# Row tiles of the router added on another engine, a gather's indices read one item early, and a first preparation over more accumulators, in a two-layer hybrid decoder step

## The chip, the cores and the metric

The kernel runs on one core of one Trainium2 chip. Its engines are TensorE (PE), VectorE (DVE), ScalarE (ACT), GpSimd (POOL) and SyncE (SP), each with a queue of its own. The metric is device time of one launch in microseconds (us), less is better; two kernels are compared in runs on the same chip.

## The reference, cut to what matters

Two decoder layers over 1024 prompt tokens and 64 sample tokens (1088 in all) of width 1024. Each layer mixes tokens, then applies a channel mixer, then adds a gated input embedding. The channel mixer of the second layer is a mixture of 8 experts of which each token takes 2, and the change lies just ahead of it and in it:

```python
def _moe_swiglu(x, w_router, wg, wu, wd):
    ...
    logits = jnp.dot(xt.astype(jnp.float32), w_router.astype(jnp.float32))
    top_v, top_i = lax.top_k(logits, TOP_K)
    top_w = jax.nn.softmax(top_v, axis=-1)
    flat_e = top_i.reshape(-1)
    order = jnp.argsort(flat_e)
    tok = order // TOP_K
    xs = xt[tok]
    sizes = jnp.bincount(flat_e, length=N_EXPERTS).astype(jnp.int32)
    h = jax.nn.silu(lax.ragged_dot(xs, wg, sizes)) * lax.ragged_dot(xs, wu, sizes)
    ys = lax.ragged_dot(h, wd, sizes) * top_w.reshape(-1)[order][:, None].astype(x.dtype)
    y = jnp.zeros_like(xt).at[tok].add(ys)
```

All arithmetic is float32. The kernel keeps an operand of a large product as two parts, a high one rounded to TensorE's faster float32 form (fp32r) and the low rest, and adds three products (high by high, low by high, high by low).

## The kernel before, in words

Activations live transposed in SBUF: `XHI` and `XLO` (high and low part) are 128 partitions by 8 column groups of the width by 1088 tokens. The five queues run on their own and meet at semaphores only; `wait_ge(sem, n)` holds the whole queue in which it stands. Each queue's order is written out by hand, layer by layer.

**Layer 0 and the mixing of layer 1** take the first half of the time. The mixer's last step in layer 1 leaves the new `XHI`, `XLO` block by block (three blocks of 384, 384 and 320 tokens, `BLOCKS`); VectorE's `finish_x` writes the last of it.

**Routing.** TensorE multiplies the three blocks by the router (`logits(0)`, `logits(1)`, then the sums of squares by `stats`, then `logits(2)`; lines 987 and 988). VectorE copies each block's logits into `LGT` (line 2271) and turns the sums into row scales in between (`norm_tokens`, lines 1725 to 1728, `scale_ready`). The same tokens are needed as rows in memory, since the experts gather them by row: for each of 9 row tiles of 128 tokens (the last has 64), GpSimd adds `XHI` and `XLO` into `XF` (line 630; 7 buffers, so the last two adds wait until earlier tiles have left, and each add counts up `xf_ready`), TensorE transposes the eight 128x128 pieces of `XF` into two PSUM banks (`rows`, line 1003), ScalarE scales them into `ROWT` (line 1495) and sends them to `token_rows` (line 1498). TensorE's order is: rows of tiles 0 and 1, logits per token (line 1017), rows 2 to 4, a wait for `counts_ready` and the running counts (lines 1024 to 1026), rows 5 to 8, the ranks of the first expert's tokens (line 1033), the list of items (line 1037). VectorE meanwhile finds the two best experts (lines 2278 to 2288), casts and compares (2291, 2294), adds up (to `counts_ready`), then finds which expert comes first (`first_known`, line 2330, on which SyncE issues the first two loads of expert weights, line 417), a mask (line 2339) and the token numbers `IDS` (`ids_ready`). When all rows are written and `IDS` is there, GpSimd gathers the first item's 336 rows in three indirect DMAs (line 635, `xg_ready`), and after that scatters the sorted token numbers to `sorted_tokens` (line 643).

**First preparation.** `prepare(k)`, for each of 8 column groups: TensorE transposes three pieces of the gathered rows `XG` into one PSUM bank (line 1051), ScalarE writes the high part `XSH` with the norm's gain as scale (line 1517), VectorE the low part `XSL` (line 2426) and frees the bank. These banks are the two miscellaneous ones (6 and 7), so TensorE is at most two groups ahead. The six main banks (0 to 5, `open_bank`, freed by `evicted`) are not used here.

**Items.** A loop of 8 items (expert by expert, 336 rows at most; the sizes of the product come from a table) does gate, up and down products: lines 704 to 706 for gate and up, 817 to 819 for down. The first product waits for each `k` of the preparation by itself (`splits`). Each item prepares the next one's rows in its last two down steps. GpSimd's loop (lines 650 to 660) fetches the rows of the item after that: it waits for `xg_used` (the preparation has read `XG`), then reads token numbers into `IDX` by three DMAs (line 656), waits for them, then gathers (line 660).

Of the kernel before, what the change touches and what calls it, by code (L numbers as in the profile page):

```python
# [18 lines left out]
F32 = mybir.dt.float32  # L19
# [3 lines left out]
ALU = mybir.AluOpType  # L23
ACT = mybir.ActivationFunctionType
AXX = mybir.AxisListType.X

P = 128
# [6 lines left out]
NT = -(-NTOK // P)  # L34
# [104 lines left out]
def build(nc, A, O):  # L139
# [5 lines left out]
    def at(name, shape, dt, off):  # L145
        return nc.alloc_sbuf_tensor_at(name, list(shape), dt, offset=off)
# [141 lines left out]
    IDX = at("IDX", [P, len(XBLK), 4], I32, PH + 80288)  # L288
    assert PH + 80336 <= END
    o = [PH + 73984]  # L290
# [72 lines left out]
    def tokens(j):  # L363
        return min(P, NTOK - j * P)
# [29 lines left out]
    def spacer(eng):  # L394

        eng.sem_inc(S["spacer"], 1)
# [132 lines left out]
    def _(g):  # L529
# [94 lines left out]

        g.wait_ge(S["split_done"], W_MOE)
        for j in range(NT):
            n = tokens(j)
            if j >= len(XF):
                g.wait_ge(S["evicted"], Q_MIX1 + 24 + 2 * (j - len(XF) + 1))
            g.tensor_tensor(XF[j % len(XF)][:, :, 0:n], XHF[:, :, j * P:j * P + n], XLF[:, :, j * P:j * P + n], ALU.add).then_inc(S["xf_ready"], 1)  # L630

        g.wait_ge(S["rows_written"], 16 * NT)
# [17 lines left out]
        with g.Fori(0, SLOTS) as it:  # L650
            with g.If(it < n_items):
                row = g.value_load(ITEMS[0:1, bass.ds(it + L_ROW + 2, 1)], min_val=0, max_val=PAIRS)
                g.wait_ge(S["xg_used"], it + 1)
                spacer(g)
                for j, (r0, n) in enumerate(XBLK):
                    g.dma_start(IDX[0:n, j, :], XS[bass.ds(row + r0, n), :]).then_inc(S["idx_ready"], 16)
                g.wait_ge(S["idx_ready"], it * 48 + 48)
                spacer(g)
                for j, (r0, n) in enumerate(XBLK):
                    g.indirect_dma_start(XG[0:n, j, :], None, XR[0:NTOK, :], bass.IndirectOffsetOnAxis(ap=IDX[0:n, j, 0:1], axis=0)  # L660
                                         ).then_inc(S["xg_ready"], 16)
# [17 lines left out]
    def _(pe):  # L679
# [166 lines left out]
        for l in range(DEPTH):  # L846
# [128 lines left out]
            else:  # L975
# [20 lines left out]
                def rows(j):  # L996

                    n = tokens(j)
                    pe.wait_ge(S["xf_ready"], j + 1)
                    for h in range(2):  # L1000
                        b = open_bank()
                        for k in range(4):
                            ins = pe.transpose(PS[0:n, b, k * P:(k + 1) * P], XF[j % len(XF)][:, 4 * h + k, 0:n], IDF[:])
                        ins.then_inc(q.next(), 1)
# [13 lines left out]
                ins.then_inc(m.next(), 1)  # L1018
                for j in range(2, 5):
                    rows(j)  # L1020
# [5 lines left out]
                pe.matmul(PS[:, b, NT * NE:(NT + 1) * NE], ONES[:], TM[:, NT - 1, :], start=True, stop=True).then_inc(m.next(), 1)  # L1026
                for j in range(5, NT):
                    rows(j)
# [94 lines left out]
                for k in range(KC):  # L1123
                    prepare(k)
                turn = nc.alloc_registers("pe_expert", engines=[pe.engine])
# [139 lines left out]
    def _(act):  # L1265
# [117 lines left out]
        for l in range(DEPTH):  # L1383
# [103 lines left out]
            else:  # L1487
# [59 lines left out]
                with nc.body("act_further", valid_engines=[act.engine]):  # L1547
# [14 lines left out]
                    act.br("act_firsts")  # L1562
                nc.switch_bb("act_firsts")
                for k in range(KC):
                    prepare(k)
                with act.Fori(0, NE) as e:
# [106 lines left out]
    def _(dve):  # L1673
# [262 lines left out]
        for l in range(DEPTH):  # L1936
# [327 lines left out]
            else:  # L2264

                for j, (t0, n) in enumerate(BLOCKS):
                    if j == 2:
                        norm_tokens()
                        dve.sem_inc(S["scale_ready"], 1)
                    ps = misc_ready()  # L2270
                    v.do(dve.tensor_copy(LGT[:, t0:t0 + n], ps[0:2 * NE, 0:n]), m)
                v.sync()
                dve.sem_inc(S["logits_ready"], 1)
                v.do(dve.memset(LG[:], 0.0))
                v.sync()
# [31 lines left out]
                assert step_ >= NT and whole is TM  # L2307
                dve.sem_inc(S["counts_ready"], 1)

                wide_e = lambda t: t.unsqueeze(1).to_broadcast([P, NT, NE])  # L2310
# [110 lines left out]

                def prepare(k):

                    dve.wait_ge(S["split_hi"], split.at(split.n + 1))
                    spacer(dve)
                    v.do(dve.scalar_tensor_tensor(XSL[:, k, :], PS[:, 6 + m.n % 2, 0:CAP], gain(3)[:, k:k + 1], XSH[:, k, :].bitcast(F32),  # L2426
                                                  ALU.mult, ALU.subtract), m)
                    v.sync()
                    dve.sem_inc(split.next(), 1)  # L2429
                    if k == KC - 1:  # L2430
                        dve.sem_inc(S["split_req"], KC)
                        sreq.n += KC
                        dve.sem_inc(S["xg_used"], 1)
# [64 lines left out]
                for k in range(KC):  # L2498
                    prepare(k)
                with dve.Fori(0, NE) as e:  # L2500
# [125 lines left out]
```

## Time and profile before, and how to read it

| what | value |
|---|---|
| median of 3 runs | 5123.61 us (5120.17 to 5128.44) |
| the profiled execution, its own time | 5115.6 us |
| its span, from first to last instruction | 5114.0 us |
| mean granted TensorE clock | 0.982 |
| PE busy, share of the span | 4951.5 us, 97% |
| DVE busy | 3363.5 us, 66% |
| ACT busy | 1587.4 us, 31% |
| POOL busy | 449.8 us, 9% |

The profiled execution is 1.6 us longer than its span, and 8.0 us under the median of the runs. Busy time leaves out waits, branches and DMA issues; a busy PE is not a PE at its peak. "Idle before" is what an engine stood still ahead of a group, with what ended that wait behind the arrow. A q behind an engine's name (SPq, ACTq, DVEq) means its queue, not its datapath. Where a time line merges several instructions of one line into one row, its duration runs from the first's start to the last's end, and short pauses are within it. The granted clock is a share of 2.4 GHz: 1.00 is 2.4 GHz, 0.50 is 1.2 GHz, and what lies between is a mean over a stretch that has both.

### The profile page before, as it was taken

To read this page: it belongs to the slowest core of one execution; us is meant where nothing else is said; L and a number is where in the kernel's file an instruction comes from. 1 tells how busy PE (TensorE), PEld (TensorE's weight loads), DVE (VectorE), ACT (ScalarE), POOL (GpSimd) and SP (SyncE) were. 2 spreads that over 40 slices of the span, in tenths; PEclk is the share of its full clock that TensorE was granted. 3 is DMA by queue.
4 is the path that set the end of the run, shared out by engine and by line. 5 is a ranking of instruction groups with operands and counts; after the bars stand their busy time and mean duration, and the time that the engine had idled before them with its cause. 6 is when DMAs were issued, how large, how long until landed. Compare 5 with 4: busy or idle time off the path is not lost.

```text
span 5114.0 us, 86952 instructions
## 1 busy us (share of the span) xinstructions
PE 4951.5 (97%) x33265; PEld 4891.5 (96%) x33266; DVE 3363.5 (66%) x5241; ACT 1587.4 (31%) x2281; POOL 449.8 (9%) x288
## 2 busy tenths in 40 slices
PE   8999999999999999999979999999999999999988
PEld 8999999999998999999969999999999999999988
DVE  5677756444556756876557777666667777876655
ACT  2112122111113311122234434333334444443333
POOL 3110101110102021110030000000000000000020
PEclk9999999999999999999989999999999999999989
DMA  3111111111111111111025554444445555554431
GB/s 105 44 45 41 41 40 42 50 41 41 49 42 44 41 56 40 47 41 42 30 89 200 173 174 164 159 143 159 152 150 194 192 184 184 190 183 155 145 128 42
DMA packets 397849, 521.90 MB, mean 102 GB/s; under 512 B 13192, under 2 KB 353654, under 8 KB 397512
## 3 DMA queue, kind: packets, MB, share of 16 engines
q1 hardware_dynamic: 358320, 459.63, 27.3%
q10 hardware_dynamic: 29272, 33.08, 1.9%
q0 software_dynamic: 9920, 24.85, 1.6%
q8 instruction: 193, 3.16, 0.3%
q14 instruction: 144, 1.18, 0.1%
HBM read 494.91 MB, written 22.60 MB: 101 GB/s over the span
## 4 chain that ended last, share of the span: by engine, by line
PE 53%; DVE 4%; issue 3%; DMA 2%; ACT 1%; DVEq 0%; ACTq 0%; POOL 0%; SPq 0%; POOLq 0%
PE PS L704 12%; PE PS L706 12%; PE PS L705 12%; PE PS L817 4%; PE PS L818 4%; PE PS L819 4%; DMA WRAW<-in_moe_w_up 1%; PE PS L1237 1%; PE PS L753 1%; PE PS L755 1%; PE PS L754 1%; ACT WHI L1285 0%; PE PS L1062 0%; DVE WLO L1685 0%; DVE XSL L2426 0%
## 5 line engine op out<-in xcount | busy, mean ns | idle before, releaser
L1685 DVE TENSOR_TENSOR WLO<-WRAW,WHI 128x1024 fp32r<-128x1024 f32 x866 | 1071.5, 1238 | 364.8 <-ACT WHI L1285 243.9
L704 PE MATMUL PS<-XHI,WHI 128*128 128x384 f32 (+1 forms) x3648 | 1203.0, 330 | 10.7 <-DVE XLO L1942 4.5
L706 PE MATMUL PS<-XHI,WLO 128*128 128x384 f32 (+1 forms) x3648 | 1197.9, 328 | 0.0
L705 PE MATMUL PS<-XLO,WHI 128*128 128x384 f32 (+1 forms) x3648 | 1196.8, 328 | 0.0
L1285 ACT ACTIVATE WHI<-WRAW 128x1024 fp32r<-128x1024 f32 x866 | 899.1, 1051 | 915.5 <-PE PS L819 604.8
L704 PE MATMUL PS<-XSH,WHI 128*128 128x232 f32 (+6 forms) x3584 | 1061.9, 296 | 13.3 <-DVEq L2429 9.9
L706 PE MATMUL PS<-XSH,WLO 128*128 128x232 f32 (+6 forms) x3584 | 1057.6, 295 | 0.0
L705 PE MATMUL PS<-XSL,WHI 128*128 128x232 f32 (+6 forms) x3584 | 1057.3, 295 | 0.0
L704 PEld LDWEIGHTS PS<-XHI,WHI 128*128 128x128 f32 x3648 | 691.7, 190 | 12.9 <-issue 5.2
L704 PEld LDWEIGHTS PS<-XSH,WHI 128*128 128x128 f32 x3584 | 681.8, 190 | 15.3 <-DVEq L2429 13.8
L705 PEld LDWEIGHTS PS<-XLO,WHI 128*128 128x128 f32 x3648 | 691.4, 190 | 0.9
L706 PEld LDWEIGHTS PS<-XHI,WLO 128*128 128x128 f32 x3648 | 690.5, 189 | 0.0
L706 PEld LDWEIGHTS PS<-XSH,WLO 128*128 128x128 f32 x3584 | 681.7, 190 | 0.0
L705 PEld LDWEIGHTS PS<-XSL,WHI 128*128 128x128 f32 x3584 | 681.4, 190 | 0.0
L817 PE MATMUL PS<-EHI,WHI 128*128 128x232 f32 (+6 forms) x1792 | 532.1, 297 | 2.8 <-DVE EACC L2477 1.7
L818 PE MATMUL PS<-ELO,WHI 128*128 128x232 f32 (+6 forms) x1792 | 524.8, 293 | 0.0
L819 PE MATMUL PS<-EHI,WLO 128*128 128x232 f32 (+6 forms) x1792 | 524.7, 293 | 0.0
L579 POOL TENSOR_TENSOR WRAW<-WRAW,PAR 128x2048 f32<-128x2048 f32 x78 | 286.2, 3670 | 2311.1 <-DMA WRAW<-in_w_in 1097.2
L2477 DVE TENSOR_TENSOR EACC<-PS,EACC 128x336 f32<-128x336 f32 x832 | 373.0, 500 | 43.0 <-PE PS L819 16.1
L1329 ACT ACTIVATE T<-T 128x384 f32<-128x384 f32 (+1 forms) x240 | 121.8, 508 | 761.7 <-DVEq L1808 761.5
L817 PEld LDWEIGHTS PS<-EHI,WHI 128*128 128x128 f32 x1792 | 338.8, 189 | 5.5 <-DVE EACC L2477 3.0
L818 PEld LDWEIGHTS PS<-ELO,WHI 128*128 128x128 f32 x1792 | 338.9, 189 | 0.0
(402 smaller groups left out, 5973.6 us busy)
## 6 DMA issues: line engine op xcount, KB each, us to landing
WRAW<-in_moe_w_gate SPq DMA_DIRECT2D x112, 1024.0 KB, 5.0
WRAW<-in_moe_w_up SPq DMA_DIRECT2D x112, 1024.0 KB, 5.0
WRAW<-in_moe_w_down SPq DMA_DIRECT2D x112, 1024.0 KB, 4.9
WRAW<-in_w_in SPq DMA_DIRECT2D x48, 1024.0 KB, 5.2
WRAW<-in_ffn_w_gate SPq DMA_DIRECT2D x11, 1024.0 KB, 5.3
WRAW<-in_ffn_w_up SPq DMA_DIRECT2D x11, 1024.0 KB, 5.3
WRAW<-in_ffn_w_down SPq DMA_DIRECT2D x11, 1024.0 KB, 5.0
expert_rows<-YT ACTq DMA_DIRECT2D x18, 512.0 KB, 3.9
```

Source lines behind the costliest of these rows:

```text
L579: g.tensor_tensor(w, w, gain(norm).unsqueeze(2).to_broadcast([P, KC, DB]), ALU.mult).then_inc(S["folded"], 1)
L704: pe.matmul(PS[:, bank, 0:n], wh, hi(k), start=(k == 0), stop=False)
L705: pe.matmul(PS[:, bank, 0:n], wh, lo(k), start=False, stop=False)
L706: ins = pe.matmul(PS[:, bank, 0:n], wl, hi(k), start=False, stop=(k == KC - 1))
L753: pe.matmul(PS[:, b, 0:n], wh[:, k, :], Y[0][:, k, t0:t0 + n], start=(k == 0), stop=False)
L817: pe.matmul(PS[:, b, 0:n], WHI[s][:, d, :], hi[:, f, t0:t0 + n], start=(f == 0), stop=False)
L818: pe.matmul(PS[:, b, 0:n], WHI[s][:, d, :], lo[:, f, t0:t0 + n], start=False, stop=False)
L819: ins = pe.matmul(PS[:, b, 0:n], WLO[s][:, d, :], hi[:, f, t0:t0 + n], start=False, stop=(f == 1))
L1285: act.activation(WHI[halves.n % HL][:], raw_view(tile % RAW, half, kind), ACT.Copy).then_inc(halves.next(), 1)
L1329: serve(lambda: act.activation(t[:, 0:n], t[:, 0:n], ACT.Sigmoid))
L1685: v.do(dve.tensor_tensor(WLO[s][:], raw_view(conv.n // 2 % RAW, conv.n % 2, kind), WHI[s][:].bitcast(F32), ALU.subtract), conv)
L2477: v.do(dve.tensor_tensor(a, ps[:, 0:CAP], a, ALU.add), q)
```

## The change

Three edits, all around the experts of layer 1.

1. The sums `XHI + XLO` for row tiles 0 to 6 leave GpSimd's queue and are formed by VectorE (`row_sums`), put between its own steps: 0 to 2 each ahead of a block's logits, 3 ahead of `norm_tokens`, 4 and 5 behind `logits_ready`, 6 behind `counts_ready`. Tiles 7 and 8 get no sum: TensorE forms each piece itself by two accumulating products with the identity, `XHI` first and then `XLO`. Rows of tile 4 move behind the running counts.
2. The first preparation uses the six main banks for groups 0 to 5 and the two miscellaneous ones for 6 and 7. ScalarE runs a one-column activation of the preparation's kind (`SCRAP`) ahead of it.
3. GpSimd's loop reads the token numbers into `IDX` as soon as the previous gather has landed, and waits for `xg_used` only ahead of the gather.

```diff
+    SCRAP = at("SCRAP", [P, 1], F32, PH + 80352)
...
@@ GpSimd
-        g.wait_ge(S["split_done"], W_MOE)
-        for j in range(NT):
-            n = tokens(j)
-            if j >= len(XF):
-                g.wait_ge(S["evicted"], Q_MIX1 + 24 + 2 * (j - len(XF) + 1))
-            g.tensor_tensor(XF[j % len(XF)][:, :, 0:n], XHF[:, :, j * P:j * P + n], XLF[:, :, j * P:j * P + n], ALU.add).then_inc(S["xf_ready"], 1)
...
-                g.wait_ge(S["xg_used"], it + 1)
+                g.wait_ge(S["xg_ready"], it * 48 + 48)
                 spacer(g)
                 for j, (r0, n) in enumerate(XBLK):
                     g.dma_start(IDX[0:n, j, :], XS[bass.ds(row + r0, n), :]).then_inc(S["idx_ready"], 16)
                 g.wait_ge(S["idx_ready"], it * 48 + 48)
+                spacer(g)
+                g.wait_ge(S["xg_used"], it + 1)
                 spacer(g)
@@ TensorE, rows
-                    pe.wait_ge(S["xf_ready"], j + 1)
+                    summed = j < len(XF)
+                    if summed:
+                        pe.wait_ge(S["xf_ready"], j + 1)
                     for h in range(2):
                         b = open_bank()
                         for k in range(4):
-                            ins = pe.transpose(PS[0:n, b, k * P:(k + 1) * P], XF[j % len(XF)][:, 4 * h + k, 0:n], IDF[:])
+                            if summed:
+                                ins = pe.transpose(PS[0:n, b, k * P:(k + 1) * P], XF[j][:, 4 * h + k, 0:n], IDF[:])
+                            else:
+                                for X in (XHI, XLO):
+                                    ins = pe.matmul(PS[0:n, b, k * P:(k + 1) * P], X[:, 4 * h + k, j * P:j * P + n], IDR[:], start=(X is XHI), stop=(X is XLO))
...
-                for j in range(2, 5):
+                for j in range(2, 4):
                     rows(j)
                 pe.wait_ge(S["counts_ready"], 1)
...
-                for j in range(5, NT):
+                for j in range(4, NT):
                     rows(j)
@@ TensorE, first preparation
                 for k in range(KC):
-                    prepare(k)
+                    if k < BANKS:
+                        b = open_bank()
+                        for j, (r0, n) in enumerate(XBLK):
+                            ins = pe.transpose(PS[:, b, r0:r0 + n], XG[0:n, j, k * P:(k + 1) * P], IDF[0:n, 0:n])
+                        ins.then_inc(q.next(), 1)
+                    else:
+                        prepare(k)
@@ ScalarE, first preparation
+                act.activation(SCRAP[:], EPSC[:], ACT.Copy, scale=gain(3)[:, 0:1])
                 for k in range(KC):
-                    prepare(k)
+                    if k < BANKS:
+                        act.wait_ge(S["mm_done"], q.at(q.n + 1))
+                        act.sem_inc(S["spacer"], 1)
+                        act.activation(XSH[:, k, :], PS[:, q.n % BANKS, 0:CAP], ACT.Copy, scale=gain(3)[:, k:k + 1]).then_inc(split.next(), 1)
+                        q.n += 1
+                    else:
+                        prepare(k)
@@ VectorE
+                def row_sums(j):
+
+                    t = slice(j * P, j * P + tokens(j))
+                    v.do(dve.tensor_tensor(XF[j][:, :, 0:tokens(j)], XHF[:, :, t], XLF[:, :, t], ALU.add), formed)
+
+                row_sums(0)
                 for j, (t0, n) in enumerate(BLOCKS):
+                    if j:
+                        row_sums(j)
                     if j == 2:
+                        row_sums(3)
                         norm_tokens()
                         dve.sem_inc(S["scale_ready"], 1)
...
                 dve.sem_inc(S["logits_ready"], 1)
+                row_sums(4)
+                row_sums(5)
                 v.do(dve.memset(LG[:], 0.0))
...
                 dve.sem_inc(S["counts_ready"], 1)
+                row_sums(6)
...
-                def prepare(k):
+                def prepare(k, main=False):
...
+                    bank, freed = (q.n % BANKS, q) if main else (6 + m.n % 2, m)
...
-                    prepare(k)
+                    prepare(k, k < BANKS)
```

## Rows read from the trace of the kernel before

**Rows 1.** Busy time by stretch: PE, PEld, DVE, ACT, POOL; then granted clock, DMA share, GB/s
```profile
2620.00:2668.50 48.50, 14.25 (x70) 11.70 (x70) 27.71 (x94) 16.77 (x25) 23.75 (x24) 0.59 0.48 155
2668.50:2672.80 4.30, 4.28 (x15) 4.29 (x16) 0.00 (x0) 2.88 (x3) 3.39 (x4) 0.50 0.04 6
2730.00:4895.00 2165.00, 2121.23 (x16049) 2111.74 (x16047) 1541.26 (x2293) 900.01 (x1166) 41.64 (x44) 0.99 0.51 169
```

**Rows 2.** Chain that ended last, last row tile to first preparation (start us, us, what)
```profile
2635.28 8.21 DMA token_rows<-ROWT
...
2647.31 8.60 DMA XG<-token_rows,IDS
```

**Rows 3.** Time line of DVE, 2604 to 2650 us (start us, us, engine, line)
```profile
2604.53 0.55 DVE L2271 COPY LGT<-PS 16x384 f32<-16x384 f32 x1 [0.23 <-DVE SQS L1713]
...
2608.57 0.17 DVE L1725 COPY RTOK<-PS 128x8 f32<-128x8 f32 x1 [1.34 <-PE PS L731]
...
2611.02 0.48 DVE L2271 COPY LGT<-PS 16x320 f32<-16x320 f32 x1 [1.58 <-PE PS L987]
...
2614.93 0.23 DVE L2278 TENSOR_TENSOR LG<-PS,RTOK 128x64 f32<-128x64 f32 x1 [3.12 <-PE PS L1017]
...
2617.30 3.42 DVE L2288 TENSOR_TENSOR TW<-MX 128x9 f32<-128x9 f32 x2
2620.88 2.17 DVE L2291 CAST IXF<-IX 128x72 f32<-128x72 uint32 x1 [0.15 <-DVE TW L2288]
2623.08 1.36 DVE L2294 TENSOR_TENSOR OH<-IOT,IXF 128x72 f32<-128x72 f32 x2
...
2627.72 0.17 DVE L2312 COPY CNT<-PS 128x8 f32<-128x8 f32 x1 [1.60 <-PE PS L1026]
...
2643.81 2.36 DVE L1685 TENSOR_TENSOR WLO<-WRAW,WHI 128x1024 fp32r<-128x1024 f32 x2 [1.07 <-issue]
...
2647.86 0.38 DVE L2413 TENSOR_TENSOR OH<-OH,TM 128x72 f32<-128x72 f32 x2
```

**Rows 4.** Time line of POOL from 2604 us
```profile
2604.39 19.82 POOL L630 TENSOR_TENSOR XF<-XHI,XLO 128x1024 f32<-128x1024 f32 x9 [98.92 <-DVE SQS L1713]
```

**Rows 5.** Time line of PE from 2610 us
```profile
2610.82 1.91 PE L1003 MATMUL PS<-IDF,XF 128*128 128x128 f32 x16
...
2626.24 0.70 PE L1024 MATMUL PS<-SS,TRIS 128*128 128x72 f32 x2 [6.98 <-DVEq L2308]
...
2627.54 5.82 PE L1003 MATMUL PS<-IDF,XF 128*128 128x128 f32 x32
```

**Rows 6.** Time line of ACT from 2628 us
```profile
2628.67 0.69 ACT L1495 ACTIVATE ROWT<-PS,RTOK 128x512 f32<-128x512 f32 x1 [7.91 <-PE PS L1003]
...
2630.61 1.30 ACT L1495 ACTIVATE ROWT<-PS,RTOK 128x512 f32<-128x512 f32 x2 [0.40 <-PE PS L1003]
...
2632.32 1.26 ACT L1495 ACTIVATE ROWT<-PS,RTOK 128x512 f32<-128x512 f32 x2 [0.40 <-PE PS L1003]
```

**Rows 7.** Time line of SP's queue from 2628 us
```profile
2630.52 0.39 SPq L417 DMA_DIRECT2D WRAW<-in_moe_w_gate  x1
```

**Rows 8.** DMA issues from 2605 to 2690 us: KB each, median us to landing
```profile
token_rows<-ROWT ACTq DMA_DIRECT2D x8, 512.0 KB, 3.7
```

**Rows 9.** Time lines of PE, ACT and DVE at the first preparation and product
```profile
2656.28 1.35 PE L1051 MATMUL PS<-IDF,XG 128*128 128x128 f32 x6 [13.89 <-DMA XG<-token_rows,IDS]
...
2668.52 0.64 PE L704 MATMUL PS<-XSH,WHI 128*128 128x336 f32 x1 [2.30 <-DVEq L2429]
...
2657.19 1.28 ACT L1517 ACT_TABLE_LOAD   x1 [10.76 <-PE PS L1051]
...
2659.17 0.57 DVE L2426 SCALAR_TENSOR_TENSOR XSL<-PS,PAR,XSH 128x336 fp32r<-128x336 f32 x1 [10.32 <-ACT XSH L1517]
2660.08 0.57 DVE L2426 SCALAR_TENSOR_TENSOR XSL<-PS,PAR,XSH 128x336 fp32r<-128x336 f32 x1 [0.34 <-DVE XSL L2426]
```

**Rows 10.** POOL's waits from 2670 to 4900 us: total, times, longest
```profile
POOL XG L660 <- DMA IDX<-sorted_tokens: 20.5, 8, 4.4
```

More of the change, by code:

```diff
@@ L288, in build @@
     IDX = at("IDX", [P, len(XBLK), 4], I32, PH + 80288)
-    assert PH + 80336 <= END
+    SCRAP = at("SCRAP", [P, 1], F32, PH + 80352)
+    assert PH + 80356 <= END
     o = [PH + 73984]
@@ L2264, in _ @@
             else:
+                formed = Count(S["xf_ready"])
+                def row_sums(j):
+                    t = slice(j * P, j * P + tokens(j))
+                    v.do(dve.tensor_tensor(XF[j][:, :, 0:tokens(j)], XHF[:, :, t], XLF[:, :, t], ALU.add), formed)
+                row_sums(0)
                 for j, (t0, n) in enumerate(BLOCKS):
+                    if j:
+                        row_sums(j)
                     if j == 2:
+                        row_sums(3)
                         norm_tokens()
@@ L2420, in _ @@
                 dve.sem_inc(S["places_ready"], 1)
-                def prepare(k):
+                def prepare(k, main=False):
                     dve.wait_ge(S["split_hi"], split.at(split.n + 1))
                     spacer(dve)
-                    v.do(dve.scalar_tensor_tensor(XSL[:, k, :], PS[:, 6 + m.n % 2, 0:CAP], gain(3)[:, k:k + 1], XSH[:, k, :].bitcast(F32),
-                                                  ALU.mult, ALU.subtract), m)
+                    bank, freed = (q.n % BANKS, q) if main else (6 + m.n % 2, m)
+                    v.do(dve.scalar_tensor_tensor(XSL[:, k, :], PS[:, bank, 0:CAP], gain(3)[:, k:k + 1], XSH[:, k, :].bitcast(F32),
+                                                  ALU.mult, ALU.subtract), freed)
                     v.sync()
```

## The prediction

> **What bounds the kernel now.** I read the busy time by stretch first. Over the items (2730 to 4895 us) TensorE is busy for 2121 of 2165 us at a clock of 0.99 [rows 1]: there the kernel is bound by TensorE, and nothing in the change takes a product away. From 2620 to 2668.5 us it is busy for only 14.25 of 48.5 us, at a mean clock of 0.59 [rows 1]. This is the serial stretch of the routing, and whatever ends it sooner moves all later work forward one for one.
>
> The chain of waits says what it consists of. The last row tile is sent at 2635.28 us and lands 8.21 us later; only then, at 2643.5, can GpSimd issue the gather; its third part, issued at 2647.31, lands 8.60 us later [rows 2]. TensorE, idle for 13.89 us, starts the first preparation at 2656.28 and the first product at 2668.52 [rows 9]. So what counts ahead of the gather is the time of the last row tile. It is late because TensorE stands for 6.98 us ahead of the running counts (line 1024) [rows 5], and ScalarE for 7.91 us ahead of tile 5 [rows 6].
>
> The time line of VectorE shows why. Two subtractions of 9 columns take 3.42 us, a cast 2.17 and two comparisons 1.36 [rows 3]; a pair of the comparisons' size takes 0.38 us later, with GpSimd at no add [rows 3]. GpSimd's nine adds fill 2604.39 to 2624.21 [rows 4], and VectorE is fast again once they are over. I read this as VectorE waiting for GpSimd's adds one by one.
>
> **Part 1, the adds leave GpSimd.** From 2617.30 to 2624.44 VectorE spends 7.14 us on these three steps. At 0.38 for each pair, 0.2 for the cast and some 0.1 for the pause they take 1.1: `counts_ready` comes 6.1 us sooner.
>
> The seven adds must find cover on VectorE. One costs 1.18 us, by the 128x1024 subtraction from SBUF, two in 2.36 [rows 3]. Sums 0 to 3 lie between 2604.3 and 2611.02. `norm_tokens` takes 2611.02 - 1.58 - 2608.57 = 0.87 us [rows 3]. Four sums (4.7), two copies of logits (1.1) and this 0.87 bring VectorE from 2604.5 to 2611.2, against 2611.02 for the third copy: 0.2 us late. TensorE is at the transposes of tiles 0 and 1 until 2612.7 [rows 5], so that costs nothing; without this cover it would cost the 0.2. Sums 4 and 5 (2.4) fit into the wait of 3.12 us ahead of line 2278, sum 6 (1.2) into that of 1.60 us ahead of line 2312 [rows 3]. Queued behind each are the short steps of the routing, for which TensorE and, over `first_known`, SyncE wait. Next late after `counts_ready` is TensorE itself.
>
> **TensorE, tiles 4 to 8.** The running counts start at 2626.24 - 6.1 = 2620.1, the rows behind them 1.3 later, 2621.4 [rows 5]. Instead of 32 transposes come 24 transposes and 32 products with the identity. No row shows such a product of 128 columns. Its bounds: 0.11 us, by 16 transposes in 1.91 at full clock [rows 5], and 0.64, by the first product of the items, which overlaps nothing at half clock [rows 9]. I take 0.18, the mean of 32 transposes in 5.82, partly at half clock [rows 5], since it too loads 128 columns and streams 128. Then the 56 end at 2631.5. ScalarE has a pace of its own: 2632.32 - 2630.61 = 1.71 us a tile, and it starts 1.13 behind TensorE [rows 5, 6]. Five tiles from 2622.5 take 4 x 1.71 + 1.3, so the last is sent at 2630.7, 4.6 earlier than before; by TensorE's pace of 0.18 at 2632.5, 2.8 earlier; with the counts and transposes at full clock (TensorE now idles 2 to 3 us ahead of them, not 7) at 2629.9, 5.4 earlier. I take 5.0, nearest to ScalarE's pace.
>
> The Trainium skill (TensorE: Matmul & The Clock Gate, Back-to-back issue gap) has about 81 ns for a pair of weight load and matmul of 128 columns. By it the 32 products would take 2.6 us and ScalarE's pace alone would decide; the transposes' 0.11 here is longer than that.
>
> **The transfers.** The last tile's 8.21 us is not its own: the median tile lands after 3.7 [rows 8]. SyncE sends the first expert weights at 2630.52, 4.8 us ahead of it [rows 2, 7]. That follows `first_known` and comes 6.1 sooner, ahead of four tiles instead of three. An added 512 KB tile costs the last one up to 3.7 us; that the weights lead by 1.1 more gives 1.1 back. I leave the 8.21 as it is; the bounds are 2.6 longer (3.7 less 1.1) and 4.5 shorter (a landing of 3.7). From the rows' landing at 2643.49 to that of the gather at 2655.91 [rows 2] it is 12.4 us; the gather shares the engines with the third load of weights in both kernels; so this stays. The first preparation starts 5.0 us sooner.
>
> **Part 2, the first preparation.** It takes 12.24 us from 2656.28 to 2668.52: two banks, so that TensorE waits for each pair to be read, and a table load of 1.28 us on ScalarE in the first [rows 9]. With eight banks TensorE waits for none. Six pieces take 1.35 with some 0.3 of run-out, so 0.2 each [rows 9]; 24 end after 5.1. Then comes the pause of 2.30 us [rows 9]. The row names VectorE's last split, but the first product needs only that of group 0; I read the pause as TensorE's own branches and reads from line 1127 on, and keep it. The product starts after 7.4 us: 4.9 gained. VectorE needs 0.57 + 0.34 = 0.91 a group [rows 9]; its first starts 1.6 after the first piece once the table load is out (2659.17 - 2656.28 - 1.28), and the eighth is done after 8.6. The product comes to group 7 after 7.4 + 7 x 3 x 0.155 = 10.7 at the least (0.29 at half clock [rows 1], halved with some rest), so it never waits. Were the pause all wait for VectorE, it would start at 5.1 and then be held to 8.6 at group 7: gain 6 to 7. Were it longer by moved code: 3.
>
> The first 15 products run at 0.50, 1.2 GHz, in 4.3 us [rows 1]. The transposes are now dense ahead of them, but for the pause. All of it at full clock would save 2.1; I take a quarter, 0.5.
>
> The one-column activation moves the table load into ScalarE's wait of 10.76 us [rows 9]. Alone it is worth nothing to the sum: with 1.28 more in front, VectorE's eighth split is done after 9.9, still ahead of 10.7. The Trainium skill (ScalarE: Activation LUTs, What ACT_TABLE_LOAD costs) counts 2.66 us a switch, drain included; the row shows 1.28 and then the activation at once. By the page the eighth split would come after 11.3 without this step, and it would be worth up to 0.6.
>
> **Part 3, indices one item early.** GpSimd waits 20.5 us in all for `IDX`, 8 times [rows 10], but TensorE waits for a gather only once, the first, which doesn't come from this loop. The rows are needed most of an item later. Three small DMAs an item move ahead of the wait; behind that wait stands only the gather. Zero.
>
> **Sum.** 5.0 + 4.9 + 0.5 = 10.4 us. The profiled execution of 5115.6 would become 5105.2; it lies 8.0 under the median of the runs, and against that median of 5123.6 I forecast 5113.2, that is 0.20% less. A measurement of this kernel can tell about 0.2%, 10.2 us, from no change, so this sits on the line.
>
> **The rivals.**
> *The row tiles stay late.* Half clock through tiles 7 and 8, or the weights ahead of the rows, leave 1 to 2 of the 5.0: 5123.6 - 1.5 - 4.9 = 5117.2. For it: the transfers overlap for 8.21 us already. Against it: TensorE would have to be slower than in any transposes of rows 5. Chance 0.2.
> *The preparation gives little.* Its groups stream, but the pause grows with the moved code or the splits hold the product: 5.0 + 2 gives 5116.6. Against it: the price of each group is in the rows. Chance 0.07.
> *All goes well.* Rows 6.1 earlier, first product at full clock: 6.1 + 4.9 + 2.1 = 13.1, 5110.5; or the pause was a wait: 5.0 + 6.5 = 11.5, 5112.1. Chance 0.2.
> *Slower: the products with the identity do not overlap.* At 0.64 each, 32 take 20.5 us, TensorE ends at 2621.4 + 4.3 + 20.5 = 2646.2, the last tile is sent at 2647.1, 11.8 late; less 4.9 that is +6.9, 5130.5. It turns slower where TensorE ends later than 2639.2, at 0.42 us a product. Against it: the products of the items, with as many weight loads, overlap. Chance 0.03.
> *It doesn't do what it says.* If GpSimd is not what slows VectorE, the 6.1 fall away and seven adds stay in the gaps: -4.9 alone, 5118.7. Chance 0.02. The forecast keeps 0.48.
>
> **Range and chances.** The likeliest is 5113.2. The cases from 5110.5 to 5118.7 hold all but the slow one; with the median's own spread of a few us the range is 5107 to 5121. Beyond the line of 10.2 us lie a little over half of the forecast (0.26) and the good case (0.2): 0.46 faster by over 0.2%. The slow case passes the line on the other side only with a product near its bound of 0.64 or with a cost that no row shows: 0.04. Within: 0.50.
>
> **What the profile after would show.** VectorE's lines 2288 to 2294 in about 1 us, and TensorE's wait ahead of line 1024 at 1 to 3 us instead of 6.98; the copy of line 2312 at about 2621.6; the last row tile sent near 2630.3; landed near 2638.5; the first product 7.4 us behind the first preparation piece, with no table load in between. I am wrong if 128-column products exceed 0.3 us, if VectorE's short steps stay slow, if the last tile takes over 10 us to land, or if the product still starts more than 9 us after the first piece.

## The result, and the profile after

The changed kernel takes 5093.81 us (median of four executions, 5088.08 to 5095.49) against 5125.71 us for the kernel before: a ratio of 0.9935, 95% interval 0.9923 to 0.9948, some 33 us or 0.65% faster. The forecast was 5113.2, the range 5107 to 5121. **It was wrong**: the sign of the likeliest case was right, but some seven tenths of the gain came from a part that I had priced at zero. The profiled execution took 5095.18 us, with a span of 5093.5. Of all runs below one execution was slow, 5369.53 us at a granted clock of 0.858 (the kernel before with its writes in pairs); its median counts it, the ratios leave it out.

TensorE's time line: start us, us, engine, line, and in brackets the idle time before and who ended it. Kernel after, the stretch of the routing:
```profile
2604.17 0.33 PE L983 MATMUL PS<-XHI,RWS 128*16 128x384 f32 x1
...
2623.37 0.70 PE L1026 MATMUL PS<-SS,TRIS 128*128 128x72 f32 x2 [2.45 <-DVEq L2336]
...
2629.54 0.28 PE L1005 MATMUL PS<-IDR,XLO 128*128 128x128 f32 x1
2629.66 0.28 PE L1005 MATMUL PS<-IDR,XHI 128*128 128x128 f32 x1
```
The first line here, the first product of the router, stood at 2600.90 in the profile before, so the earlier layers ran 3.27 us longer in this execution. Counted from it, the running counts start 19.20 us later, against 25.34 before [rows 5], 6.1 sooner, and the first preparation (2654.11, below) 49.94 later against 55.38 [rows 9], 5.4 sooner. The products with the identity start 0.11 to 0.14 us apart (16 of them fill 2629.40 to 2631.22, at a granted clock of 1.00); I had priced them at 0.18.

VectorE's time line of the kernel after, same stretch:
```profile
2614.92 2.36 DVE L2286 TENSOR_TENSOR XF<-XHI,XLO 128x1024 f32<-128x1024 f32 x2
...
2618.20 0.22 DVE L2306 TENSOR_TENSOR LG<-PS,RTOK 128x64 f32<-128x64 f32 x1 [0.84 <-PE PS L1019]
...
2620.57 0.24 DVE L2316 TENSOR_TENSOR TW<-MX 128x9 f32<-128x9 f32 x2
2620.97 0.20 DVE L2319 CAST IXF<-IX 128x72 f32<-128x72 uint32 x1 [0.15 <-DVE TW L2316]
2621.20 0.38 DVE L2322 TENSOR_TENSOR OH<-IOT,IXF 128x72 f32<-128x72 f32 x2
```
The three slow steps of [rows 3] (3.42, 2.17 and 1.36 us) take 0.24, 0.20 and 0.38. Behind the sums VectorE still waits for TensorE (0.24, 0.84 and 0.22 us ahead of the third copy of logits, of line 2306 and of line 2341), so they cost nothing.

Now the first product. TensorE's time line of the kernel after, from the preparation on:
```profile
2654.11 3.62 PE L1129 MATMUL PS<-IDF,XG 128*128 128x128 f32 x18 [14.45 <-DMA XG<-token_rows,IDS]
2657.52 1.33 PE L1053 MATMUL PS<-IDF,XG 128*128 128x128 f32 x6
...
2661.80 0.42 PE L700 MATMUL PS<-XSH,WHI 128*128 128x336 f32 x1 [0.55 <-DVEq L2459]
...
2667.47 0.65 PE L700 MATMUL PS<-XSH,WHI 128*128 128x336 f32 x1 [4.93 <-DVEq L2459]
...
2673.82 0.65 PE L700 MATMUL PS<-XSH,WHI 128*128 128x336 f32 x1 [5.15 <-DVEq L2459]
...
2688.74 1.03 PE L1064 MATMUL PS<-IDF,EACC 128*128 128x128 f32 x8
```
ScalarE's time line, same kernel and stretch:
```profile
2655.06 1.66 ACT L1577 ACTIVATE XSH<-PS,PAR 128x336 fp32r<-128x336 f32 x3 [7.12 <-issue]
2657.47 0.54 ACT L1577 ACTIVATE XSH<-PS,PAR 128x336 fp32r<-128x336 f32 x1 [0.75 <-PE PS L1129]
2660.43 0.54 ACT L1577 ACTIVATE XSH<-PS,PAR 128x336 fp32r<-128x336 f32 x1 [2.42 <-remote]
2666.10 0.54 ACT L1577 ACTIVATE XSH<-PS,PAR 128x336 fp32r<-128x336 f32 x1 [5.12 <-remote]
2672.46 0.54 ACT L1525 ACTIVATE XSH<-PS,PAR 128x336 fp32r<-128x336 f32 x1 [5.82 <-remote]
```
The product starts at 2658.58, only 4.5 us after the first piece (7.4 foretold, 12.24 before). But it doesn't run through: it waits twice for some 5 us for a split of VectorE. VectorE waits for ScalarE, and ScalarE for TensorE's transposes, all of which were over at 2658.85: the sixth group is read at 2666.10, the seventh at 2672.46. What is late are TensorE's increments of the semaphore ("remote": the wait ended with an increment beside which the trace has no instruction's end). The trace records the sixth at 2665.99 and the seventh at 2672.35, 8.3 and 14.1 us after the ends of their transposes at 2657.73 and 2658.29. In the profile before all eight stand 0.01 to 0.02 us behind those ends, and the products ran from 2668.52 to `item_out`'s transposes (of the item's results, ahead of their way to memory) at 2686.75, 18.2 us; here it is 30.2. The 7.8 us that edit 2 won ahead of the product are lost behind its start, and 4.2 more.

The gain stands in the items. First and last transposes of `item_out` in TensorE's time line, kernel before:
```profile
2686.75 1.03 PE L1062 MATMUL PS<-IDF,EACC 128*128 128x128 f32 x8
...
4894.19 1.22 PE L1062 MATMUL PS<-IDF,EACC 128*128 128x128 f32 x8 [3.80 <-DVE EACC L2477]
```
The last ones in the kernel after (the first stood above):
```profile
4874.18 1.09 PE L1064 MATMUL PS<-IDF,EACC 128*128 128x128 f32 x8 [3.79 <-DVE EACC L2507]
```
From one to the other it is 2207.4 us before and 2185.4 after (from 2688.74), 22.0 less. TensorE's waits in the items, kernel before (total, times, longest):
```profile
PE PS L1062 <- DVE YT L2442: 20.2, 6, 5.1
```
The same view of the kernel after:
```profile
PE PS L1064 <- DVE YT L2472: 2.6, 3, 1.4
```
Behind that wait stands a load. The time line of SyncE's queue at the start of the second item, kernel before:
```profile
2925.32 0.37 SPq L417 DMA_DIRECT2D WRAW<-in_moe_w_gate  x1
2936.04 0.37 SPq L417 DMA_DIRECT2D WRAW<-in_moe_w_up  x1
```
GpSimd's there:
```profile
2933.11 1.00 POOL L660 DMA_INDIRECT XG<-token_rows,IDX  x1 [2.35 <-DMA IDX<-sorted_tokens]
...
2935.69 1.10 POOL L660 DMA_INDIRECT XG<-token_rows,IDX  x1 [0.30 <-issue]
```
And ScalarE's:
```profile
2945.50 1.06 ACT L1285 ACTIVATE WHI<-WRAW 128x1024 fp32r<-128x1024 f32 x1 [5.74 <-DMA WRAW<-in_moe_w_up]
```
The three parts of the gather are issued from 2933.11 to 2935.69, the load of `up` weights at 2936.04. The load lands after 9.3 us instead of the usual 5.0; I read this as the gather and the load sharing the DMA engines. ScalarE waits 5.74 us for it, and 3.13 us reach TensorE at 2951.16. The same time lines of the kernel after, SyncE's queue first:
```profile
2926.90 0.37 SPq L418 DMA_DIRECT2D WRAW<-in_moe_w_gate  x1
2936.99 0.37 SPq L418 DMA_DIRECT2D WRAW<-in_moe_w_up  x1
```
GpSimd's:
```profile
2930.64 1.00 POOL L656 DMA_INDIRECT XG<-token_rows,IDX  x1 [231.50 <-DVEq L2463]
...
2933.22 0.90 POOL L656 DMA_INDIRECT XG<-token_rows,IDX  x1 [0.30 <-issue]
```
ScalarE's:
```profile
2943.28 1.06 ACT L1293 ACTIVATE WHI<-WRAW 128x1024 fp32r<-128x1024 f32 x1 [2.58 <-DMA WRAW<-in_moe_w_up]
```
Before, the numbers were asked for at 2929.02, once `XG` was free, and the gather followed 4.1 us later; now it starts as `XG` comes free, 2.5 us sooner by the traces' times and 4.1 counted from there. So it falls into the 10 us in which SyncE issues no load, and is mostly done when the `up` load comes, which lands after 6.2 us. TensorE no longer waits ahead of these transposes.

### The profile page after: what moved, and what is told of

Same layout as the page of the kernel before. It is cut to its first block, busy times and chain, and to the rows that moved or that the text cites. A ratio compares the mean times of both kernels' runs of the same rounds, so it can differ in the third digit from the quotient of the medians.

```text
span 5093.5 us, 86982 instructions
## 1 busy us (share of the span) xinstructions
PE 4948.4 (97%) x33281; PEld 4890.4 (96%) x33282; DVE 3365.5 (66%) x5248; ACT 1588.2 (31%) x2282; POOL 425.4 (8%) x279
## 4 chain that ended last, share of the span: by engine, by line
PE 52%; DVE 4%; issue 3%; DMA 2%; ACT 1%; DVEq 0%; ACTq 0%; POOL 0%; another core or an unknown queue 0%; SPq 0%; POOLq 0%
PE PS L700 12%; PE PS L701 12%; PE PS L702 12%; PE PS L813 4%; PE PS L814 4%; PE PS L815 4%; DMA WRAW<-in_moe_w_gate 1%; DVE EACC L2507 1%; PE PS L1245 1%; PE PS L749 1%; PE PS L750 1%; PE PS L751 1%; DVE WLO L1700 1%; ACT WHI L1293 0%; PE PS L1064 0%
## 5 line engine op out<-in xcount | busy, mean ns | idle before, releaser
L2507 DVE TENSOR_TENSOR EACC<-PS,EACC 128x336 f32<-128x336 f32 x832 | 372.7, 499 | 43.1 <-PE PS L815 15.3
```

The source lines that it names most:

```text
L2507: v.do(dve.tensor_tensor(a, ps[:, 0:CAP], a, ALU.add), q)
```

## The experiments

Times are medians; the interval is that of the ratio to the kernel before on the same chip.

**Each edit alone.** The kernel before took 5124.85 us (23 executions).

Edit 3 alone:
```diff
-                g.wait_ge(S["xg_used"], it + 1)
+                g.wait_ge(S["xg_ready"], it * 48 + 48)
                 spacer(g)
                 ...
                 g.wait_ge(S["idx_ready"], it * 48 + 48)
+                spacer(g)
+                g.wait_ge(S["xg_used"], it + 1)
```


> The kernel before with edit 3 alone: the token numbers of the next item are read one item early. Theory A (the gather of each item, which this starts about 2.5 us sooner, no longer holds up the load of up weights that follows it): the items become 20 to 25 us shorter in sum, the time falls by 20 to 25 us against the kernel before, and ScalarE's waits for WRAW of the up weights fall from 44 us to under 15. Theory B (the whole gain comes from the stretch of the routing, edits 1 and 2, as the prediction's sum had it): 0 us, and the waits stay.

Measured 5102.33 us, ratio 0.9955 (0.9942 to 0.9968): 23 us faster, as theory A has it. ScalarE's waits for `up` weights fall from 44.1 us (9 waits, longest 6.5) to 15.3 (7, longest 4.1; "under 15" was just missed), and TensorE's ahead of `item_out`:
```profile
PE PS L1064 <- DVE YT L2444: 3.7, 4, 1.4
```

Edit 1 alone:
```diff
-        for j in range(NT):
-            ...
-            g.tensor_tensor(XF[j % len(XF)][:, :, 0:n], XHF[...], XLF[...], ALU.add).then_inc(S["xf_ready"], 1)
+                row_sums(0)
+                ...
+                                for X in (XHI, XLO):
+                                    ins = pe.matmul(PS[...], X[...], IDR[:], start=(X is XHI), stop=(X is XLO))
```


> The kernel before with edit 1 alone: row sums on VectorE, tiles 4 and 5 ahead of the counts only up to tile 3, the last tiles formed by identity products on TensorE. Theory A: 4 to 6 us faster (the last row tile sent 4.5 to 5 us sooner counted from the first logits product) and nothing more. Theory B (this edit has the gain, by something that I missed): 20 us or more faster.

Measured 5117.21 us, ratio 0.9991 (0.9982 to 1.0000): 4.6 us by the ratio, 7.6 by the medians. The first preparation starts 49.0 us behind the router's first product against 55.4. In the seven profiles without edit 1 it is 53.5 to 55.4, in the nine with it 48.6 to 49.9 but for one of 44.6, so this distance has some 2 us of play of its own. Theory A, with little room for anything else.

Edit 2 alone:
```diff
-                    prepare(k)
+                    if k < BANKS:
+                        b = open_bank()
+                        ...
+                act.activation(SCRAP[:], EPSC[:], ACT.Copy, scale=gain(3)[:, 0:1])
```


> The kernel before with edit 2 alone: the first six pieces of the first preparation into the six main accumulators, and the table load ahead of them. The prediction's sum: 4.9 us faster. Theory C (the profile of the kernel after shows the first product early, but held inside it by the splits of later groups, 5 us each for the sixth and seventh): 0 to 2 us faster.

Measured 5127.58 us, ratio 1.0003 (0.9994 to 1.0011): nothing. TensorE's waits from 2660 to 2698 us show the same holds inside the product:
```profile
PE PS L705 <- DVEq L2444: 12.1, 3, 5.2
```

The whole change beside them:

> The whole change once more on the same chip as the three parts. 28 to 33 us faster than the kernel before. If the parts are independent, their three gains add up to this one within 3 us.

Measured 5096.37 us, ratio 0.9946 (0.9933 to 0.9959): 28 us. By the ratios the parts give 23.1 + 4.6 - 1.5 = 26.2, within the 3 us.

**Where the gather may lie.** Two kernels move it the other way; the kernel before took 5124.46 us.
```diff
                 g.wait_ge(S["idx_ready"], it * 48 + 48)
                 spacer(g)
+                g.wait_ge(S["ys_out"], it * 48 + 48)
+                spacer(g)
                 for j, (r0, n) in enumerate(XBLK):
                     g.indirect_dma_start(XG[0:n, j, :], ...
```


> The kernel before, with one more wait ahead of each item's gather (not of the reading of the token numbers): GpSimd waits until ScalarE's three transfers of the previous item's results have landed, some 35 us into the item instead of 6. Theory A1 (edit 3 gains because the gather no longer runs at the same time as the first up weights of the item, whichever way it is moved): 20 to 25 us faster, ScalarE's and VectorE's waits for those weights and TensorE's 20 us ahead of the item_out transposes go as they did with edit 3. Theory A2 (what gains is that the transfers of the gather or the numbers come earlier as such; later is worse, since the gather meets other loads there): 0, or slower by up to 20 us.

Measured 5119.81 us, ratio 0.9994 (0.9985 to 1.0003): 3 us, not 20, and the interval holds no change. The waits that A1 named went: ScalarE's for `up` weights are 8.6 us in all, TensorE's ahead of `item_out` 1.8. As the token numbers are read when they were before, it is the gather itself that held up these loads. The time did not go, since other waits took their place. A line of ScalarE's waits in the items:
```profile
ACT WHI L1287 <- DMA WRAW<-in_moe_w_gate: 61.8, 45, 7.6
```
And one of TensorE's:
```profile
PE PS L819 <- DVE EACC L2479: 17.2, 5, 5.6
```
Issued from 2979.08 on, the gather meets a `gate` load issued at 2982.25. The wait has a new name and is nearly as long.

```diff
-                g.wait_ge(S["idx_ready"], it * 48 + 48)
+                g.wait_ge(S["idx_ready"], it * 96 + 48)
+                spacer(g)
+                for j, (r0, n) in enumerate(XBLK):
+                    g.dma_start(IDX[0:n, j, :], XS[bass.ds(row + r0, n), :]).then_inc(S["idx_ready"], 16)
+                g.wait_ge(S["idx_ready"], it * 96 + 96)
```


> The kernel before, with the three reads of the token numbers made twice, one after the other: each gather is issued 3 to 4 us later than before. Theory A1 (overlap with the load of up weights, issued 3 to 4 us behind the gather's start, decides): the gather now starts at or behind the up load; the load has less in front of it, so the items get 0 to 15 us shorter in sum, or stay; if the gather still shares the engines with the up load all through, 0 to 10 us slower. Theory A2 (earlier is better): 20 us slower.

Measured 5111.42 us, ratio 0.9972 (0.9963 to 0.9981): 14 us faster, with more work and a later gather. "Earlier is better" (A2) falls. The gather now starts just behind the `up` load (2945.33 against 2944.60), so ScalarE waits for `down` weights instead, 60.0 us against 30.5 before (its waits in the items):
```profile
ACT WHI L1289 <- DMA WRAW<-in_moe_w_down: 60.0, 50, 6.0
```
TensorE waits ahead of `item_out` for half as long as the 20.2 us before:
```profile
PE PS L1066 <- DVE YT L2446: 9.7, 6, 3.5
```
Counted from the moment at which `XG` is free, the gather of the second item starts after 4.1 us in the kernel before, at once with edit 3, after 7.7 us (2945.33 less 2937.59) with the second read and after 35.8 (2979.08 less 2943.25) when held. Against before that gives, by the ratios: 4.1 sooner, -23 us; 3.7 later, -14; 31.7 later, -3. What counts is which load the gather meets. Stretches of 10 us without an issue of one lie only around the start of an item; in the kernel before the loads further on in the second item come every 6 to 7.5 us, and 5.0 is the usual time from issue to landing.

**Why edit 2 gives nothing.** While the first preparation runs, GpSimd issues 18 indirect writes of 16 bytes a row (`sorted_tokens`), one each 1.3 us. Theories D and E ask whether these writes are what makes the increments late. Two kernels hold them until the first preparation has used `XG`; the kernel before took 5124.46 us:
```diff
         g.wait_ge(S["places_ready"], 1)
+        spacer(g)
+        g.wait_ge(S["xg_used"], 1)
+        spacer(g)
         for j in range(NT):
```


> The kernel before, with GpSimd's 18 scattered writes of the sorted tokens held until the first preparation has used XG. Theory D (these writes delay TensorE's semaphore increments in that stretch; the first product waits up to 4 us for the last split in some executions): 3 to 6 us faster, and the time of the quicker runs of the kernel before (5115 to 5118) becomes the usual one. Theory E (the late increments come from the weight loads or from TensorE's own queue, not from these writes): 0.

Measured 5130.69 us, ratio 1.0012 (1.0003 to 1.0021): 6 us slower. Its first `item_out` starts 43.4 us after the first piece of the preparation, against 30.5 in the profile before: the writes now lie beside the first products, and a copy of VectorE there waits 10.65 us for a late increment.

> The changed kernel with the same hold of the 18 scattered writes. Theory D: the first product, begun 4.5 us after the first piece, no longer waits 4 to 5 us each for the sixth and later splits; 8 to 11 us faster than the changed kernel, that is 36 to 40 us faster than the kernel before, and edit 2 gets its gain of about 5 us (difference of this and of the same hold in the kernel before, less the 27 to 28 of edits 1 and 3). Theory E: as the changed kernel, 28 us faster than before, with the same waits inside the first product.

Measured 5100.03 us, ratio 0.9962 (0.9949 to 0.9976): 19 us faster than the kernel before, some 8 less than the change. The forecast of a gain fell, but in the traces the delay goes with the writes, as theory D has it. In this second kernel no product waits for a split for more than 0.17 us, and `item_out` starts 21.9 us after the first piece (2672.3 less 2650.38) instead of 34.6. But the products behind this `item_out` are now torn by pauses of up to 1.3 us, 7.0 in all, and from here to the second item's `item_out` it takes 274.0 us instead of 256.6; the two stretches together are 295.9 us against 291.3. These pauses have no releaser in the view ("issue"). So late increments are not shown to be behind them: the writes may hold up TensorE in a second way. TensorE's time line there:
```profile
2681.77 0.38 PE L704 MATMUL PS<-XSL,WHI 128*128 128x264 f32 x1 [1.31 <-issue]
2683.89 0.38 PE L704 MATMUL PS<-XSL,WHI 128*128 128x264 f32 x1 [1.29 <-issue]
```

So I spread the writes instead of moving them: in pairs, each once those before have landed. The kernel before took 5126.94 us beside the next two.
```diff
         for j in range(NT):
             n = tokens(j)
+            g.wait_ge(S["scattered"], 16 * (len(XBLK) + 2 * j))
+            spacer(g)
             for k in range(2):
                 g.indirect_dma_start(XS[0:PAIRS, :], ...
```


> The changed kernel with the 18 scattered writes of the sorted tokens sent in pairs, each pair only once all before it have landed; they end some 20 us later than now. Theory D1 (it is the pile of these small writes, up to several in flight, that delays TensorE's semaphore increments): the splits' waits inside the first product go, and edit 2 shows its 5 us or more: 5 to 10 us faster than the changed kernel, 33 to 38 faster than the kernel before. Theory D2 (any such write in flight delays them; only its place in time counts, as the two runs with the writes held suggest, where the late increments moved with them): as the changed kernel or up to 5 us slower, and late increments for a longer time. Theory E (not these writes): as the changed kernel.

Measured 5085.33 us, ratio 0.9918 (0.9904 to 0.9931): 42 us faster than the kernel before, as theory D1 has it, and 4 more than its upper bound.

> The kernel before with the same pairing. Theory D1: 2 to 5 us faster than the kernel before, which then has no wait for splits inside its first product. Theory D2 and theory E: 0 to 5 us slower.

Measured 5125.71 us, ratio 0.9996 (0.9986 to 1.0005): nothing; D1's 2 to 5 us did not come, though no wait for a split is left inside its first product.

**The two by two.** Edit 2 out or in, the writes as they are or in pairs, on one chip (the kernel before took 5120.68 us). The edits are those above; the first two kernels have edits 1 and 3.

> Edits 1 and 3 without edit 2. Theory F (edit 2 is worth nothing as long as the scattered writes hold the splits of the first product): 27 to 28 us faster than the kernel before, as the whole change. The prediction's sum for edit 2: 5 us less of a gain, 22 to 23 us.

> Edits 1 and 3 without edit 2, with the scattered writes in pairs. Theory F: 5 us slower than the whole change with the pairs (35 to 37 us faster than the kernel before against 41), since nothing holds the first product there and edit 2 starts it 5 us sooner. Rival G (the pairs gain by themselves, and edit 2 still adds nothing): the same as the whole change with the pairs.

> The whole change on the same chip, as a measure for the three beside it: 27 to 32 us faster than the kernel before.

> The whole change with the scattered writes in pairs, again. 38 to 44 us faster than the kernel before if the first measurement holds, that is 8 to 14 us faster than the whole change.

| | writes as they are | writes in pairs |
|---|---|---|
| without edit 2 | 5095.98 us, 0.9942 (0.9929 to 0.9956) | 5092.26 us, 0.9940 (0.9927 to 0.9953) |
| with edit 2 | 5097.97 us, 0.9952 (0.9939 to 0.9965) | 5082.46 us, 0.9924 (0.9911 to 0.9937) |

With the writes as they are edit 2 gives nothing (2 us the wrong way by the medians). With the writes in pairs it gives 9.8 us by the medians and 8.2 by the ratios; the intervals overlap, but all five times with it (5081.86 to 5086.51) lie under all five without (5088.16 to 5101.60). So edit 2 pays only with the pairs, as theory F has it. Its sizes missed: 5 us for edit 2 were too few, the pairs without edit 2 gave 28 to 31 us instead of 35 to 37, and the whole change 23 to 25 here instead of 27 to 32. TensorE's time line with the pairs and without edit 2:
```profile
2655.73 1.35 PE L1054 MATMUL PS<-IDF,XG 128*128 128x128 f32 x6 [13.42 <-DMA XG<-token_rows,IDS]
...
2667.98 0.64 PE L701 MATMUL PS<-XSH,WHI 128*128 128x336 f32 x1 [2.31 <-DVEq L2446]
...
2686.33 1.04 PE L1065 MATMUL PS<-IDF,EACC 128*128 128x128 f32 x8
```
With the pairs and with edit 2:
```profile
2652.63 3.62 PE L1131 MATMUL PS<-IDF,XG 128*128 128x128 f32 x18 [13.13 <-DMA XG<-token_rows,IDS]
...
2660.34 0.42 PE L702 MATMUL PS<-XSH,WHI 128*128 128x336 f32 x1 [0.17 <-issue]
...
2674.46 0.71 PE L1066 MATMUL PS<-IDF,EACC 128*128 128x128 f32 x5
```
From first piece to `item_out` it is 30.6 us and 21.8. Of these 8.8 us 7.9 lie ahead of the product. Most of the rest is the clock: over the first 4 us of the products the granted clock is 0.50 in the first kernel and 1.00 in the second, in which the transposes stand right ahead of them. ScalarE's time line of the second shows it read six pieces in one run:
```profile
2653.58 3.33 ACT L1579 ACTIVATE XSH<-PS,PAR 128x336 fp32r<-128x336 f32 x6 [6.18 <-PE PS L1131]
```
Why the pairs give nothing without edit 2 stands in the same profiles. They bring the first `item_out` from 36.3 us after the first piece to 30.6, but from there to the second item's it takes 261.7 us instead of 256.5: together 292.3 against 292.8. The spread writes end late, so the second item's gather is issued from 2725.30 on instead of from 2687.20, and it meets a `gate` load, which lands after 8.5 us (time lines of GpSimd, SyncE's queue, ScalarE and TensorE, with the pairs and without edit 2):
```profile
2725.30 1.03 POOL L657 DMA_INDIRECT XG<-token_rows,IDX  x1 [7.01 <-DMA IDX<-sorted_tokens]
...
2728.72 0.37 SPq L417 DMA_DIRECT2D WRAW<-in_moe_w_gate  x1
...
2737.37 1.06 ACT L1288 ACTIVATE WHI<-WRAW 128x1024 fp32r<-128x1024 f32 x1 [5.96 <-DMA WRAW<-in_moe_w_gate]
...
2740.84 0.57 PE L814 MATMUL PS<-EHI,WHI 128*128 128x264 f32 x1 [3.44 <-DVE EACC L2494]
```
I read this as the same collision in another place; it takes back 3.4 of the 5.2 us. With edit 2, too, the pairs cost TensorE a wait there (2.58 us), but they win 15.3 us ahead of it (21.8 us from first piece to `item_out` against 37.2).

The change with the writes in pairs is the best version here: 39 and 42 us faster than the kernel before in two measurements, 8 to 16 faster than the change (5085.33 against 5093.81 in different batches, 5082.46 against 5097.97 on one chip).

## Why the prediction was wrong

- **Part 1 was right.** `counts_ready` was to come 6.1 us sooner: 6.1, from the counts' start. The last row tile 5.0 sooner: it is sent at 2634.08, 29.91 behind the router's first product against 34.38, so 4.5. It lands after 7.41 us (8.21 was kept), and the first preparation starts 5.4 sooner (5.0). Edit 1 alone gave 4.6. That sum and measurement meet this well is in part luck, as this distance varies by some 2 us between profiles.
- **Part 2 failed at "so it never waits".** I took VectorE's pace of 0.91 us a group and let the eighth split be done after 8.6 us; it came after 20.5 (2674.61 less 2654.11), since TensorE's semaphore increments were late. So the 4.9 were nothing. I had also kept the pause of 2.30 us as TensorE's branches, with 7.4 us to the product; it was 4.5, as the product follows the transposes without a pause. And I had taken 0.5 of the 2.1 us that full clock would save; undisturbed (the change with the pairs), the first products run at 1.00. With the writes in pairs the edit is worth 8 to 10, more than any case of mine.
- **Part 3 failed at "Zero", and that decides.** I argued that the gathered rows are needed most of an item later, which holds, and that behind GpSimd's wait stands only the gather. I asked who waits for the gather, not what the gather is in the way of. The profile of the kernel before had it: TensorE's 20.2 us ahead of `item_out`, and ScalarE's 44.1 us for `up` weights in 9 waits, of up to 6.5 us. Moving the gather 4.1 us was worth 23.
- **The ground of the sum.** In the profile before the product ran through without late splits. In all nine other profiles with unpaced writes beside the first preparation, edit 2 in or out, piece to `item_out` took 34.6 to 38.5 us, against its 30.5. So it did not show a cost that the other profiles carry. Its time of 5115.6 us is also one of the lowest (the 23 executions beside the single edits lie at 5115.4 to 5131.5), but that the one goes with the other is not shown: with the pairs and without late splits a profiled execution of the kernel before took 5129.85.
- Of the rivals, "the preparation gives little" named the right place ("the splits hold the product") at 0.07. None had a gain in the items.

## What to carry to other kernels

When a transfer moves in time, list what it then runs beside, as well as who waits for it: a gather that nobody waits for can hold up a load on which the bound engine has no slack, and here 4 us decided it. Try both directions and a far place, since the gain here was not a matter of early or late. And if an edit that must gain by the rows gives nothing, look for what holds the next step: here pacing the small writes took the hold away, and the edit paid. But look then at what the paced transfers push back in their turn.

## What the runs showed of the hardware

- While many small indirect writes were in flight, TensorE's semaphore increments came late, in the profile after by up to 14.1 us, though the instructions' own times were normal. The delay moved when the writes were moved, and the waits went when they were sent in pairs. How the writes cause it is open, and so is whether the pauses of TensorE without a releaser (7.0 us with the writes held) have the same cause. The Trainium skill (SBUF — State Buffer, SBUF: two separate sides) says that a DMA cannot be slowed by a compute operation nor the other way round. The operations themselves weren't slowed here, but the waits between engines grew, and that costs the same. Some records of semaphores are missing from the traces in these stretches, so a single delay is less sure than the idle time of TensorE.
- Products of 128 columns with a new weight load each took 0.11 us at full clock, as the transposes do. The Trainium skill (TensorE: Matmul & The Clock Gate, Back-to-back issue gap) has 81 ns for this; the trace is longer, and the difference cost nothing, since ScalarE, at 1.67 us a tile, did not wait for these products.
- Issued right behind a gather of three parts, a 1 MB load landed after 9.3 us instead of the usual 5.0; with the gather 4.1 us sooner it landed after 6.2.
- While GpSimd added tiles of 128x1024 from SBUF, two 9-column subtractions of VectorE took 3.42 us and a cast 2.17 [rows 3]; without those adds they took 0.24 and 0.20.
- What did not get settled: some 1.8 of the 5.2 us that the pairs give back in the first item without edit 2, and why the profile before has no late increments where nine others do. The one-column activation was not tried alone.
